# Row vectors and modulations by TensorE, four rankings beside the scores, a shorter candidate list, 64 gathered rows summed by TensorE

## The reference: what is computed

```
mod = silu(c) @ ada_w + ada_b                # 6 vectors of 1024, and 2 more for the final norm
hn  = rmsnorm(x) * g * (1 + sc1) + sh1       # token-wise norm, modulation by channel
proj = hn @ w_in                             # 28 column tiles of 128
o_h = 4 heads of a gated recurrence, both directions
o_c = silu(layernorm(depthwise_conv31(a * sigmoid(gate)) + bias))     # 512 channels
h   = x + g1 * (concat(o_h, o_c) @ w_out)
hn2 = rmsnorm(h) * g * (1 + sc2) + sh2
# PEER: 8 heads, 128 x 128 experts, 16 chosen for each token and head
s1, s2 = scores against two sets of 128 keys
v1, i1 = top_k(s1, 16); v2, i2 = top_k(s2, 16)
cand   = v1[:, None] + v2[None, :]           # 16 x 16 sums
sc, ci = top_k(cand, 16)
e = i1[ci // 16] * 128 + i2[ci % 16]; w = softmax(sc)
y = sum_j (w_j * gelu(hn2 . u[e_j])) * v[e_j]      # 128 experts for each token
out = rmsnorm(h + g2 * y) * (1 + fsc) + fsh
```

## Time and profile before

| what | value |
|---|---|
| median of three runs | 3498.98 us |
| the profiled execution | 3496.35 us, its span 3494.6 us |
| busy in the span: TensorE, VectorE, ScalarE, GpSimd | 80%, 75%, 17%, 41% |
| mean granted TensorE clock | 0.896 of full |
| read from and written to HBM | 821.82 MB, 87.56 MB |

### The profile page before, as it was taken

The page is one execution under the profiler, slowest core; times in us unless marked ns, Lnnn a source line. Parts: engine busy times, 40 slices in busy tenths (PEclk is TensorE's granted clock), DMA queues, the critical chain, the costliest instruction groups (busy, mean ns, idle before and its releaser), DMA issues. The chain is left out here.

```text
span 3494.6 us, 30341 instructions
## 1 busy us (share of the span) xinstructions
PE 2780.6 (80%) x10012; PEld 1577.4 (45%) x10012; DVE 2614.9 (75%) x4271; ACT 582.9 (17%) x639; POOL 1420.4 (41%) x1168
## 2 busy tenths in 40 slices
PE   2623799876699896688787887998699999999895
PEld 1522577764488642343443443453344433343332
DVE  6799845551344799999999999986677777677777
ACT  2321343331311100121221211121000000000003
POOL 4774311112211245333333334545455545555552
PEclk6866799888899897899898999999899999999998
DMA  3441111002222499788888789999999999999996
GB/s 159 135 136 60 48 43 37 31 31 81 92 81 72 156 369 363 266 294 322 280 303 325 262 316 338 381 415 410 399 403 400 403 401 401 403 399 400 398 390 230
DMA packets 297085, 911.21 MB, mean 261 GB/s; under 512 B 26864, under 2 KB 76272, under 8 KB 293616
## 3 DMA queue, kind: packets, MB, share of 16 engines
q0 software_dynamic: 147456, 536.94, 40.6%
q1 hardware_dynamic: 111104, 293.37, 23.0%
q10 hardware_dynamic: 38384, 79.18, 6.1%
HBM read 821.82 MB, written 87.56 MB: 260 GB/s over the span
## 5 line engine op out<-in xcount | busy, mean ns | idle before, releaser
L1423 PE MATMUL s_pu<-s_hn,s_ut 128*128 128x512 f32 x2048 | 919.8, 607 | 27.5 <-ACT s_gst L1507 27.5
L1699 DVE SCALAR_TENSOR_TENSOR s_hB<-s_slot,s_dot,s_hB 128x1024 f32<-128x1024 f32 x508 | 648.2, 1285 | 263.2 <-DMA s_slot<-in_v,s_row 262.1
L1387 POOL DMA_INDIRECT s_slot<-in_u,s_row x512 | 515.2, 1006 | 764.3 <-DVE s_slot L1688 649.1
L1387 POOL DMA_INDIRECT s_slot<-in_v,s_row x512 | 545.5, 1065 | 467.1 <-DVE s_hB L1699 404.9
L1688 DVE SCALAR_TENSOR_TENSOR s_slot<-s_slot,s_ph 128x1024 f32<-128x1024 f32 x512 | 604.3, 1219 | 50.5 <-DMA s_slot<-in_u,s_row 32.5
L1423 PEld LDWEIGHTS s_pu<-s_hn,s_ut 128*128 128x128 f32 x2048 | 395.2, 196 | 500.0 <-issue 500.0
L300 PE MATMUL s_ps<-hn_hi,w_hi 128*128 128x512 f32 x832 | 344.8, 414 | 229.5 <-DVE s_hp L518 121.5
L1483 PE MATMUL s_pw<-s_ct,s_vt 128*128 128x512 f32 x512 | 257.7, 628 | 98.5 <-DVE s_ct L1707 94.5
L301 PE MATMUL s_ps<-hn_lo,w_hi 128*128 128x512 f32 x832 | 336.0, 404 | 0.0
L300 PEld LDWEIGHTS s_ps<-hn_hi,w_hi 128*128 128x128 f32 x832 | 163.9, 197 | 272.9 <-issue 175.7
L524 DVE SCALAR_TENSOR_TENSOR s_work<-s_hp,s_tap,s_work 128x1024 f32<-128x1024 f32 x116 | 261.9, 2258 | 8.7
(11 more groups left out here) (264 smaller groups left out, 2925.3 us busy)
## 6 DMA issues: line engine op xcount, KB each, us to landing
s_ut<-in_u_tiles SPq DMA_DIRECT2D x128, 512.0 KB, 7.2
s_vt<-in_v SPq DMA_DIRECT2D x128, 512.0 KB, 25.6
s_g<-s_gst ACTq DMA_DIRECT2D x128, 256.0 KB, 6.9
s_w<-s_wb ACTq DMA_DIRECT2D x16, 2048.0 KB, 8.5
s_gr<-s_g SPq DMA_DIRECT2D x64, 512.0 KB, 26.0
s_wr<-s_w SPq DMA_DIRECT2D x16, 2048.0 KB, 33.7
s_ada<-in_ada SPq DMA_DIRECT2D x48, 512.0 KB, 3.7
s_x<-in_xT SPq DMA_DIRECT2D x16, 512.0 KB, 4.3
```

What stands on the lines that cost most here:

```text
L1387: pool.indirect_dma_start(out=slot[s][:, :], out_offset=None, in_=io[kind], in_offset=bass.IndirectOffsetOnAxis(ap=row[b][:, j:j + 1], axi ...
L1423: mm = pe.matmul(pu[:, n % 2, :], ut[n % UR][:, k, :], hn[:, k, :], start=(k == 0), stop=(k == DC - 1))
L1699: dve.scalar_tensor_tensor(y, s, dot[b][:, j:j + 1], y, ALU.mult, ALU.add).then_inc(taken, 1)
```

## The change

**Stages 1 and 2.** The modulation sums are made by TensorE: `cact` (128x1) is held and each piece of `ada_w` streams through, so that a row 1x1024 grows in PSUM; ScalarE copies it out, and products with one row turn it into columns. `accumulate`, `scale_rows` and `add_rows` go, GpSimd keeps only the `w_lo` remainders, and the multiplication by r moves to VectorE. The loops of stage 2 are written out. The ring for `ada_w` rows has 5 slots in place of 3, and the 48 column products stand ahead of the layer norm's sums.

```diff
 
         @block.gpsimd
         def _(pool):
-            pool.wait_ge(r_ready, 1)
-            for k in range(DC):
-                pool.tensor_tensor(x[:, k, :], x[:, k, :], r[:, :], ALU.mult).then_inc(xn_ready, 1)
...
-            for k in range(DC - LO_POOL, DC):
-                pool.wait_ge(hi_ready, k + 1)
-                pool.tensor_tensor(m.hn_lo[:, :, k, :], two(x[:, k, :]), m.hn_hi[:, :, k, :].bitcast(F32), ALU.subtract)
...
+            pe.wait_ge(cact_done, 1)
             for v in range(2):
-                pe.wait_ge(acc_ready, v + 1)
+                pe.wait_ge(ada_in[2 * v], 16)
+                pe.wait_ge(ada_in[2 * v + 1], 16)
+                for k in range(DC):
+                    for h in range(2):
+                        c = slice(h * HALF, (h + 1) * HALF)
+                        mm = pe.matmul(ps_row[v][0:1, c], m.cact[:, k:k + 1], ada[:, v, k, c],
+                                       start=(k == 0), stop=(k == DC - 1))
+                mm.then_inc(row_ready, 1)
+            for v in range(2):
+                pe.wait_ge(row_taken, v + 1)
                 for c in range(DC):
-                    pe.matmul(ps_mod[:, v * DC + c:v * DC + c + 1], acc[:, v, c * P:(c + 1) * P], m.ones[:, 0:1],
+                    pe.matmul(ps_mod[:, v * DC + c:v * DC + c + 1], rows[0:1, v, c * P:(c + 1) * P], m.ones[0:1, 0:1],
                               start=True, stop=True)
             pe.drain().then_inc(mod_ready, 1)
...
-            def accumulate(v):
-                for k in range(DC):
...
-                    dve.drain()
-                dve.drain().then_inc(acc_ready, 1)
...
+            dve.wait_ge(r_ready, 1)
+            for k in range(DC):
+                dve.tensor_tensor(x[:, k, :], x[:, k, :], r[:, :], ALU.mult)
             dve.wait_ge(mod_ready, 1)
...
         @block.gpsimd
         def _(pool):
-            pool.memset(vec[:, :, :], 0.0)
...
+            for c in range(1, CONV_C + 3):
                 for s in range(2):
                     w.remainder(pool, c, s)
...
-            def add_rows(c, items):
-                for i in items:
...
-                    pool.wait_ge(prod_ready, c * A_PER + i + 1)
-                    pool.tensor_tensor(vec[:, i % 6, :], vec[:, i % 6, :], prod[:, i % 2, :], ALU.add)\
-                        .then_inc(prod_used, 1)
...
+            def ada_rows(items):
+                for n in items:
+                    v, k = divmod(n, DC)
+                    pe.wait_ge(ada_in[n % A_SLOTS], 16 * (n // A_SLOTS + 1))
+                    if k == 0 and v >= 2:
+                        pe.wait_ge(row_taken, v - 1)
+                    for h in range(2):
+                        c = slice(h * HALF, (h + 1) * HALF)
+                        mm = pe.matmul((ps_mu, ps_var)[v % 2][0:1, c], m.cact[:, k:k + 1], ada[:, n % A_SLOTS, c],
+                                       start=(k == 0), stop=(k == DC - 1))
+                    mm.then_inc(ada_used, 1)
+                    if k == DC - 1:
+                        pe.drain().then_inc(row_ready, 1)
+
-            with pe.Fori(0, CONV_C) as c:
...
+                ada_rows(range(c * A_PER, (c + 1) * A_PER))
...
+            pe.wait_ge(row_taken, 6)
+            for v in range(6):
+                for c in range(DC):
+                    pe.matmul(ps_var[:, v * DC + c:v * DC + c + 1], vec[0:1, v, c * P:(c + 1) * P], m.ones[0:1, 0:1],
+                              start=True, stop=True)
+            pe.drain().then_inc(mod_ready, 1)
```

```diff
                 act.wait_ge(xn_ready, k + 1)
-                act.activation(h1[:, k, :], h1[:, k, :], ACT.Identity, scale=m.mods[:, 4, k:k + 1],
-                               bias=m.mods[:, 3, k:k + 1])
-                act.drain()
-                act.activation(m.hn_hi[:, :, k, :], two(h1[:, k, :]), ACT.Copy).then_inc(y_hi, 1)
...
+                act.activation(m.hn_hi[:, :, k, :], two(y[:, k, :]), ACT.Identity, bias=m.mods[:, 3, k:k + 1])\
+                   .then_inc(y_hi, 1)
...
-            dve.wait_ge(stored, 16 * DC)
...
+            def remainder(k):
+                dve.wait_ge(y_hi, k + 1)
+                dve.scalar_tensor_tensor(m.hn_lo[:, :, k, :], two(y[:, k, :]), m.mods[:, 3, k:k + 1],
+                                         m.hn_hi[:, :, k, :].bitcast(F32), ALU.add, ALU.subtract)
...
-                dve.tensor_tensor(h1[:, k, :], h1[:, k, :], r[:, :], ALU.mult).then_inc(xn_ready, 1)
...
+                dve.scalar_tensor_tensor(y[:, k, :], h1[:, k, :], m.mods[:, 4, k:k + 1], r[:, :], ALU.mult, ALU.mult)\
+                   .then_inc(xn_ready, 1)
+                if k >= 2:
+                    remainder(k - 2)
```

```diff
-                for b in range(2):
+                for i in range(MADE_PICKS):
                     for part in range(3):
-                        m.picks[b].part(dve, h, part, sc[:, :, b, :])
+                        m.picks[i].part(dve, h, part, sc[:, :, RANKED[i], :])
...
+CAND_RANGES = ((0, 1, 16), (1, 4, 8), (4, 8, 4), (8, 16, 1))
+CANDS = sum((a1 - a0) * nb for a0, a1, nb in CAND_RANGES)
...
-        dve.tensor_tensor(self.cand[:, :, :], self.val[:, 2 * h, :].unsqueeze(2).broadcast_to([P, TOPK, TOPK]),
-                          self.val[:, 2 * h + 1, :].unsqueeze(1).broadcast_to([P, TOPK, TOPK]), ALU.add)
+        at = 0
+        for a0, a1, nb in CAND_RANGES:
+            na = a1 - a0
+            dve.tensor_tensor(self.cand[:, at:at + na * nb].rearrange("p (a b) -> p a b", a=na),
+                              self.val[:, 2 * h, a0:a1].unsqueeze(2).broadcast_to([P, na, nb]),
+                              self.val[:, 2 * h + 1, 0:nb].unsqueeze(1).broadcast_to([P, na, nb]), ALU.add)
+            at += na * nb
...
-                dve.tensor_scalar(half[0][:, :], flat, 4, None, ALU.logical_shift_right)
-                dve.tensor_scalar(half[1][:, :], flat, 15, None, ALU.bitwise_and)
+                for s in range(2):
+                    dve.tensor_scalar(half[s][:, :], flat, 3 - s, None, ALU.logical_shift_right)
                 dve.tensor_copy(keyf[:, :, :], pk.key[:, :, :])
+                dve.tensor_copy(part[2][:, :], flat)
...
+                a, x, p, y = (t[:, :] for t in part)
+                dve.tensor_scalar(a, a, -1.0, 0.0, ALU.add, ALU.max)
+                dve.drain()
+                dve.scalar_tensor_tensor(a, x, -6.0, a, ALU.add, ALU.max)
+                dve.drain()
+                dve.scalar_tensor_tensor(a, p, -48.0, a, ALU.add, ALU.max)
+                dve.drain()
+                dve.tensor_scalar(x, a, 8.0, 8.0, ALU.mult, ALU.add)
+                dve.tensor_scalar(y, a, 4.0, 24.0, ALU.mult, ALU.add)
+                dve.tensor_copy(halff[0][:, :], a)
+                dve.drain()
+                dve.scalar_tensor_tensor(x, a, 16.0, x, ALU.mult, ALU.min)
+                dve.scalar_tensor_tensor(y, a, 48.0, y, ALU.add, ALU.min)
+                dve.drain()
+                dve.tensor_tensor(x, x, y, ALU.min)
+                dve.drain()
+                dve.tensor_tensor(halff[1][:, :], p, x, ALU.subtract)
+                dve.drain()
...
-                        dve.wait_ge(sc_in, 16 * (i - 1))
-                    m.picks[i % 2].part(dve, x // 3, x % 3, sc[:, x // 3 * 2:x // 3 * 2 + 2, :])
+                        dve.wait_ge(sc_in[i % 2], 16 * ((i - MADE_PICKS) // 2 + 1))
+                    m.picks[i % MADE_PICKS].part(dve, x // 3, x % 3, sc[i % 2][:, x // 3 * 2:x // 3 * 2 + 2, :])
...
+                if b == 0 and j == SIDE_ROWS:
+                    dve.wait_ge(y_taken, 1)
...
-            for x in range(24, 32):
-                ranking(1, x)
...
+                        if done == P + 8:
+                            coefficients(0)
...
+            dve.wait_ge(side_done, SIDE_ROWS)
```

```diff
-RANKED = (0, 1, 4, 5, 2, 6, 3, 7)
+RANKED = (0, 1, 4, 5, 6, 2, 7, 3)
+MADE_PICKS = 4
 DENSE = (4, 5, 6, 7)
-RING = 10
+RING = 8
+SIDE = 2
+SIDE_ROWS = 64
...
+    m -= SPARSE * P
+    if m < SPARSE * (P - SIDE_ROWS):
+        i, b = divmod(m, SPARSE)
+        return "v", b, i + (0 if b else SIDE_ROWS)
+    i, b = divmod(m - SPARSE * (P - SIDE_ROWS), SPARSE - 1)
+    return "v", 1 + b, P - SIDE_ROWS + i
...
+SPARSE_OPS = 2 * SPARSE * P - SIDE_ROWS
+RANK_AT, RANK_TILES, LAST_STEPS = 12, 20, 4
+HOT_AT = (10, 38, 66, 94)
+HOT_TILES = 24
+SIDE_AT, SIDE_TILES = 46, 78
...
+def rank_tile(i, x):
+
+
+    if i < MADE_PICKS:
+        return (i - 1) * LAST_STEPS + (x - 24) * LAST_STEPS // 8
+    return RANK_AT + (i - MADE_PICKS) * RANK_TILES + x * RANK_TILES // 32
...
+    return [(i, x) for i in range(1, len(RANKED)) for x in range(24 if i < MADE_PICKS else 0, 32) if rank_tile(i, x) == n]
...
-    done = 0
+    tenths = 0
...
+        tenths += 44 if t < HOT_AT[0] else 34 if t < RANK_AT + RANK_TILES * (len(RANKED) - MADE_PICKS) else 51
+    return tenths // 10
...
+def side_tile(j):
+    return SIDE_AT + j * SIDE_TILES // SIDE_ROWS
...
+                for i in range(MADE_PICKS, len(RANKED)):
```

(30 more changed lines are left out.)

252 lines of the change are left out of this document (105 added, 147 removed).

## The result

The changed kernel takes **3317.18 us** (median of 3 runs, 3316.27 to 3320.53), where the kernel before takes 3498.98: ratio 0.9482, with a 95% interval of 0.946 to 0.9503. The forecast was 3310, the range 3240 to 3390. The profiled execution has a span of 3318.8 us, 175.8 less than before.

A forecast was written before the change was run, and what follows sets the result against it. It took VectorE's convolution to bound stage 2, and VectorE until about 2230, then DMA, to bound stage 6. Gains 6 + 97 + 3 - 8 + 90 = 188 off 3496.35 gave 3308, forecast as 3310, range 3240 to 3390.

The forecast's parts named there:

- Stage 1: Modulation sums as 32 row products on TensorE, ending near 84 us in place of 89.6: gain 6.
- rival A: Row products of stages 1 and 2 run at half clock: 3408 us, chance 0.07.
- Stage 2: Convolution freed of GpSimd: four blocks 184 us in place of 288, gain 104, less 10, plus 3: 97.
- three projections (33): Stage 2: TensorE's projections left behind the last convolution's start, 33 us of the 60 until the sums are ready.
- The comparison of 42.7 with 46: Stage 2, per channel block: TensorE's 42.7 us of projections and row products fit beside VectorE's 46.
- 10 lost: End of stage 2: sums ready 60 us after the last convolution's start, where the old order would give 50.
- Stages 3 to 5: Stage 4 gains 3 us; in stage 5 the four rankings' steps behind the last head lose 8.
- 155 of 209, hidden behind TensorE: Stage 5: VectorE's total with four rankings' steps added, 155 of 209 us, claimed to cost nothing before the last head.
- Stage 6: VectorE, then TensorE, then from tile 92 DMA lead; gain 102 us, less 12 for small waits: 90.
- Rival C: Middle of the u stretch not smooth, tiles 12 to 91 at 10 us in place of 9.1: 3383 us, chance 0.17.
- Rival D: Better: DMA holds 412 GB/s (31 us less) and no friction (12 less): 3267 us, chance 0.22.
- Rival B: Stage 2's convolution does not speed up, blocks stay at 61.5 us: 3372 us, chance 0.05.

The follow-up runs named there:

- experiments 1: The changed kernel with stages 1 and 2 as in the kernel before (row sums by VectorE, ScalarE and GpSimd): 3400.17 us.
- experiment 2: The changed kernel with 32 GpSimd adds of [128 x 1024] f32 in stage 2 that feed nothing: 3361.52 us.
- experiment 9: The kernel before with 64 candidate sums in place of 256 and nothing else changed, so other experts are fetched: 3447.76 us.
- experiment 6: The changed kernel with fewer side rows in place of 64: with 32, 3324.54 us; with 8, 3345.49 us.
- 7: The changed kernel with VectorE doing the last six u takes between the fourth and fifth product of the v stretch: 3315.63 us.
- 8: The changed kernel loading only the first eight v tiles for the dense blocks and reusing them, 63 MB less: 3287.37 us.
- experiment 3: The changed kernel with stage 2's 48 column products behind the variance sums and the additions to `mods` last: 3298.63 us.
- experiment 5: The changed kernel with the column products late and five rankings, in place of four, made with the scores in stage 5: 3319.45 us.
- 4: The changed kernel with two rankings in place of four made with the scores, the other six in the u stretch: 3347.81 us.

## Why the prediction was right, and where it was off

**What bounds the kernel.** Right: VectorE's convolution in stage 2, slowed by GpSimd (experiments 1 and 2), VectorE in the u stretch (experiment 9: nearly each us off it there was a us off the time) and the transfers behind it (6, 7 and 8).

**Stage 1: 13.8 in place of 6.** The price of a row product was right, and rival A is out: with one column held and 512 streamed the clock is full. Two terms of the sum were too large: the products start at 26.9, not near 30, and the 16 column products take 3.7, not 7.1, because the clock stood at 1.00 behind the row products, where the earlier trace rows had been taken at 0.50. The rows held make no difference: at a clock of 0.57 a column product took 0.381 with 128 rows (18.31 for 48, the kernel before at 419.83) and 0.378 with one (experiment 3).

**Stage 2: 71 in place of 97.** This is the one step that failed, by two terms. The first, 9 us: a block was set at 46 and takes 48.2. The two weight remainders beside it were put at 2.5 together; in the second block the 29 passes take 43.25 in place of 39.15, 4.1 for two remainders. From the prediction's own rows (3.10 against 1.35 per add) it could have been 3.5. The second, 17 us: "three projections (33)" behind the start of the last convolution. TensorE had more left: at 246.3, when that block starts, 6.6 us of row products and four projections, 43.8. With 16.2 of column products and 9.9 of sums this makes the 77 us measured, in place of 60. The comparison of 42.7 with 46 had said that TensorE keeps up, and it does: from 77.7 to 313.2 it waits about 1 us in all. But it begins its first row products at 102.4, when VectorE begins the first block (102.6), and gets ahead only by what its blocks are shorter, 14 us in three. By the prediction's own numbers that lead is 3 x 3.3 = 9.9, and what is left behind the last start is 20.8 - 9.9 + 4 x 10.9 = 54.5, not 33. Experiment 3 prices the order: 18.6 us of the forecast were to be had by leaving the column products in the tail, where VectorE works anyway. The prediction saw this cost (10 lost) and left out TensorE's late start.

**Stages 3 to 5: -6.2 in place of -8.** The heads are 25.3 apart, as foretold. The closing part takes 1119.43 - 1101.78 = 17.65, forecast 17.9. But "155 of 209, hidden behind TensorE" was nearer its end than the text had it: VectorE's room was some 2 us a head (experiment 5). Its busy time is not all that it needs: in a head of 25.34 us after it is busy 21.05 and waits 1.92 for scores, and the other 2.4 are gaps between instructions. By that sum a fifth ranking would have cost the 5 of its tail; it cost 34.

**Stage 6: 97.7 in place of 93.** By the gelus of the tiles ahead of them, tile 12 begins 102 us after the loop's start (120 forecast), tile 46 after 408 (422), tile 92 after 841 (847). From there the transfers took 1291 us at 400 GB/s, 516 MB; the forecast had 514 MB at 402, 1279, and 12 of friction. VectorE led where it was to lead, TensorE from tile 46 to 92, the transfers from tile 92. Rival C, a rough middle, did not come; nor did E, in which each side row costs a full wait: TensorE waited 31.9 us for 64 of them, 0.5 each. Rival D, 412 GB/s to the end, held for the u stretch alone (413, then 394 and 392). The v stretch gave 47, where the prediction looked for some 60, and the u stretch the other 47. Rival B is out by experiment 2.

What the stage's parts are worth, each taken by itself: 64 candidates 48.5 (9, on the kernel before), two more rankings in stage 5 30.6 (4), 56 of the 64 side rows 28.3 (6). They come to 107 against 97.7, but do not stand on one base, and the longer closing part, 3.05 each, is in none of them. That the sum hit so well owes something to errors of both signs: +8 in stage 1, -26 in stage 2, +6 behind them.

Left open: how much of the 7 us that 32 side rows fewer cost, against 21 for the next 24, is more than spread. The first had the 11 us to use up by which the takes were early, and with 8 TensorE waits 62 us more for VectorE's weights than after (experiment 6); whether that is all of the difference was not tried.

## What to carry to other kernels

Before TensorE is given work beside a VectorE loop, follow it to the loop's end and ask how late its queue stands there, not only whether its total fits; then put what nothing waits for behind what something does. A GpSimd operation that reads SBUF beside VectorE passes with two SBUF inputs costs about one such pass and a half (2.1 us against 1.29): moving it to an engine that is busier can still win. And where the transfers are saturated, price a change by when it lets the bytes start: there, waits removed from the engines come back as waits for DMA (experiments 6 and 7).

## What the runs showed of the hardware

- A GpSimd add [128 x 1024] f32 and a VectorE pass with two SBUF inputs go in step: 3.2 to 3.3 us for the pair, against 1.3 for the pass alone. GpSimd pays too: its adds take 2.39 us ahead of the passes and 3.30 beside them (experiment 2). Of nine remainders beside the passes of after four took 3.26 to 3.46 and five 2.34 to 2.77, so a lone one does not always pay.
- An f32 product with one column held and 512 streamed takes 0.863 us, as one with 128 columns (0.865), and the granted clock stays at 1.0 (2.4 GHz) through 27.5 us of them. One-row column products take 0.233 us each right behind them (clock 1.0), and 0.338 and 0.378 where the clock was 0.65 and 0.57 (after, at 297 to 313, and experiment 3). With 128 rows they took 0.446 at 0.50 and 0.381 at 0.57 (the kernel before): the price follows the clock, not the rows.
- The transfers reached 400 GB/s as a mean of 1291 us and 413 over 331 us, on one core.
